# One core, two transformer blocks: the first stage in another order, and two modulation pieces summed by TensorE

## What is computed

```python
cond = jax.nn.silu(c)
mod = (cond @ w_ada[l] + b_ada[l])[:, None, :]
sh1, sc1, g1, sh2, sc2, g2 = jnp.split(mod, N_MOD, axis=-1)
h = x * (1.0 + sc1) + sh1
z = h @ w_in[l] + b_in[l]
z_u, z_v, z_h, z_g = jnp.split(z, split_pts, axis=-1)
```

## Time and profile before

| | |
|---|---|
| median of 3 executions | 2645.43 us (2644.23 to 2646.96) |
| profiled execution, its own time | 2642.59 us |
| its span, first to last instruction | 2641.3 us |
| TensorE busy, share of the span | 98% |
| VectorE / ScalarE busy | 70% / 49% |
| mean DMA rate over the span | 227 GB/s |
| mean granted TensorE clock | 0.995 |

### The profile page before, as it was taken

One profiled execution on the slowest core, in us unless ns is written; L12 is line 12 of the kernel. 1 busy time (PEld: TensorE's weight loads), 2 busy tenths in 40 slices (PEclk: granted clock), 3 DMA queues, 4 the chain that ended last, 5 costly groups with the idle time before them and its releaser, 6 DMA issues.

```text
span 2641.3 us, 31620 instructions
## 1 busy us (share of the span) xinstructions
PE 2599.3 (98%) x12546; PEld 2172.6 (82%) x12546; DVE 1846.0 (70%) x1927; ACT 1290.1 (49%) x1566; POOL 32.1 (1%) x55
## 2 busy tenths in 40 slices
PE   7899999999999999999999999999999999999999
PEld 3689988878888888888888888888888888988887
DVE  7879899988876644577776767755554665656565
ACT  2345544444444444555555544444444654555463
POOL 0000000000000000000000000000000000000000
PEclk9899999999999999999999999999999999999999
DMA  8998878798788755665656555555656556634554
GB/s 346 360 376 321 299 274 320 261 318 327 271 270 276 262 190 180 198 208 196 194 191 205 180 189 185 183 191 191 210 186 196 182 191 168 176 126 158 195 176 143
DMA packets 276584, 598.65 MB, mean 227 GB/s; under 512 B 21264, under 2 KB 46288, under 8 KB 260064
## 3 DMA queue, kind: packets, MB, share of 16 engines
q1 hardware_dynamic: 268272, 566.52, 63.1%
q0 software_dynamic: 4560, 21.56, 2.5%
q10 hardware_dynamic: 3616, 8.68, 0.9%
HBM read 586.24 MB, written 10.49 MB: 226 GB/s over the span
## 4 chain that ended last, share of the span: by engine, by line
PE 92%; DVE 5%; ACT 1%; DMA 1%; issue 1%; ACTq 0%; SPq 0%; DVEq 0%
PE ps L925 26%; PE ps L927 26%; PE ps L926 26%; PE ps L1050 2%; PE ps L1034 2%; PE ps L1036 2%; PE ps L1037 2%; DVE w_lo L2238 1%; DVE group_acc L2357 1%; DMA raw<-in_w_in 1%; PE ps L1433 1%; PE ps L1434 1%; PE ps L1435 1%; PE ps L1092 1%; PE ps L1085 0%
## 5 line engine op out<-in xcount | busy, mean ns | idle before, releaser
L2238 DVE TENSOR_TENSOR w_lo<-raw,w_hi 128x1024 fp32r<-128x1024 f32 x870 | 1050.3, 1221 | 673.2 <-ACT w_hi L1579 671.4
L1579 ACT CAST w_hi<-raw 128x1024 fp32r<-128x1024 f32 x870 | 906.6, 1051 | 1050.0 <-PE ps L927 913.3
L925 PE MATMUL ps<-w_lo,x_hi 128*128 128x512 f32 x2592 | 1021.2, 394 | 4.3 <-DVE w_lo L2238 2.8
L927 PE MATMUL ps<-w_hi,x_lo 128*128 128x512 f32 x2592 | 1011.6, 390 | 0.0
L926 PE MATMUL ps<-w_hi,x_hi 128*128 128x512 f32 x2592 | 1011.1, 390 | 0.0
L925 PEld LDWEIGHTS ps<-w_lo,x_hi 128*128 128x128 f32 x2592 | 488.3, 188 | 107.8 <-DVE w_lo L2238 4.6
L927 PEld LDWEIGHTS ps<-w_hi,x_lo 128*128 128x128 f32 x2592 | 488.1, 188 | 102.9
L926 PEld LDWEIGHTS ps<-w_hi,x_hi 128*128 128x128 f32 x2592 | 488.7, 189 | 100.3 <-issue 1.4
L2266 DVE SCALAR_TENSOR_TENSOR ada_acc<-raw,cond,ada_acc 128x2048 f32<-128x2048 f32 x64 | 150.1, 2345 | 2.0 <-DMA raw<-in_w_ada 1.0
L925 PE MATMUL ps<-w_lo,pooled_hi 128*128 128x512 f32 x384 | 150.2, 391 | 0.0
L927 PE MATMUL ps<-w_hi,pooled_lo 128*128 128x512 f32 x384 | 149.5, 389 | 0.0
(11 more groups left out here) (379 smaller groups left out, 2136.6 us busy)
## 6 DMA issues: line engine op xcount, KB each, us to landing
raw<-in_w_m SPq DMA_DIRECT2D x128, 1024.0 KB, 5.3
raw<-in_w_ada SPq DMA_DIRECT2D x64, 1024.0 KB, 5.7
raw<-in_pool_w_in SPq DMA_DIRECT2D x64, 1024.0 KB, 5.4
raw<-in_w_in SPq DMA_DIRECT2D x56, 1024.0 KB, 7.5
raw<-in_k_mod SPq DMA_DIRECT2D x32, 1024.0 KB, 6.6
raw<-in_pool_w_out SPq DMA_DIRECT2D x32, 1024.0 KB, 5.0
raw<-in_ple_w_gate SPq DMA_DIRECT2D x32, 1024.0 KB, 5.1
raw<-in_mla_w_in SPq DMA_DIRECT2D x24, 1024.0 KB, 5.1
```

Source lines behind the costliest of these rows:

```text
L925: mm(bank, xh, wl, start=start, stop=False)
L927: ins = mm(bank, xl, wh, start=False, stop=stop)
L1579: nc.scalar.copy(by_ktile(st, w_hi[st.half_slot(j, half)][:, 0:n]), raw_half(st, j, half)).then_inc(hi_split, 1)
L2238: tt(by_ktile(st, w_lo[slot][:, 0:n]), raw_half(st, j, half), by_ktile(st, w_hi[slot][:, 0:n].bitcast(F32)), ALU.subtract).then_inc(lo_spl ...
```

## The change

Three things change.

Pieces (1,2) and (2,6) are no longer added by VectorE. Their letter becomes `p`, and TensorE multiplies the landed data itself: `raw_block` is one single-column product of a 128x128 block with a column of `cond`, and 16 of them make a piece. The 16 of piece (1,2) stand between the products of unit (0,0), eight in each half, one after each of the first two products of a tile and k. Those of piece (2,6) stand in the second half of unit (1,1), two at each such place. They accumulate in the bank and columns of `group_sum`, whose products then add to them. The load four places behind a `p` waits for a new semaphore, `raw_summed`.

The banks of the filter products are spread (`spec_bank`), so that fewer of them wait for a copy. On TensorE the third filter's second part, the fourth filter and `group_sum(1)` change places: the sum comes first, and both parts of the fourth filter stand between the halves of units (0,2), (1,0) and (1,1). On VectorE `filter_part(3,0)` moves behind `group_sum(1)`, `filter_part(3,1)` behind the rest of unit (1,2), and the rest of unit (2,0) behind `group_scale(2)`. On ScalarE the rounding of unit (0,1) moves ahead of a spectrum copy.

Three of the four spectrum stores move from the end of the stage to where each spectrum is copied, the two first Gelus move into `in_h`, and on VectorE one modulation load and one output (`vu_third`) do so too.

```diff
@@ -121,7 +121,7 @@
 STREAM = [
-    ("first", 1, [("ggggggggw", ""), ("ggwggwggggw", ""), ("ggwggwggggw", ""), ("ggwggwgwgwgg", "wwww")]),
+    ("first", 1, [("ggggggggw", ""), ("ggwpgwggggw", ""), ("ggwggwggpgw", ""), ("ggwggwgwgwgg", "wwww")]),
     ("in_vu", 1, [("w", "aa")]), ("in_h", 2, A2), ("in_h2", 1, [("wwa", "wwaa")] * 2), ("in_g", 4, [("wwaa", "wwaa"), ("ww", "ww")]),
@@ -134,6 +134,9 @@
 FIRST_W = [(0, 0), (0, 1), (0, 2), (1, 0), (1, 1), (1, 2), (2, 0), (2, 1), (0, 3), (1, 3), (2, 2), (2, 3), (3, 0), (3, 1), (3, 2)]
+RAW_PIECE = (None, 2, 6, None)
@@ -415,6 +418,7 @@
     group_added = sem("group_added")
+    raw_summed = sem("raw_summed")
     ident_in = sem("ident_in")
@@ -547,16 +551,19 @@
     def group_ada(q, u):
-        return nth_load("g", 8 * q + u)
+        return [j for j, of in enumerate(ST["first"].pattern) if of != "w"][8 * q + u]
+    def added_by(q, u):
+        return sum(n != RAW_PIECE[p] for p in range(q + 1) for n in range(u if p == q else 8))
     def first_half(q, c, half):
...
     def spec_bank(it, m):
-        return 6 if it > 1 else 2 * m if it else 4 + 2 * m
+        return (2 * m, 4 + 2 * m, 2 + 2 * m, 6)[it]
     def sum_bank(q):
-        return 6 if q else 4
+        return 6 if q else 0
     WIDE = ("w_o", "m2", "pool_out", "w_out", "gate1")
@@ -599,8 +606,11 @@
                 used_g = st.freed("g", i, j)
+                used_p = st.freed("p", i, j)
                 if used_g > 0:
                     sync.wait_ge(group_added, used_g)
+                if used_p > 0:
+                    sync.wait_ge(raw_summed, used_p)
             if isinstance(src, tuple):
@@ -909,7 +919,7 @@
         mm = nc.tensor.matmul
-        def products(st, i, j, half, kt, hi, lo, banks, first, last, tiles=(0, 1)):
+        def products(st, i, j, half, kt, hi, lo, banks, first, last, tiles=(0, 1), between=None):
             slot = st.half_slot(j, half)
@@ -923,7 +933,11 @@
                     mm(bank, xh, wl, start=start, stop=False)
+                    if between:
+                        between(4 * c + 2 * t)
                     mm(bank, xh, wh, start=False, stop=False)
+                    if between:
+                        between(4 * c + 2 * t + 1)
                     ins = mm(bank, xl, wh, start=False, stop=stop)
@@ -1078,7 +1092,7 @@
             if it > 1:
-                pe.wait_ge(spec_copied, 2 * it + d)
+                pe.wait_ge(spec_copied, (2, 3, 4, 7)[2 * it + d - 4])
             for t in range(2):
@@ -1093,25 +1107,37 @@
             ins.then_inc(spec_mm, 1)
+        def raw_block(q, e, n):
+            st, u = ST["first"], RAW_PIECE[q]
+            j = group_ada(q, u)
+            col = e * 2 * CH + n * P
+            if e + n == 0:
+                pe.wait_ge(raw_full[st.slot(j)], st.landed(0, j))
+            ins = mm(ps[:, sum_bank(q), n:n + 1], raw[st.slot(j)][:, col:col + P], cond[:, 2 * u + e:2 * u + e + 1],
+                     start=e + n == 0, stop=False, skip_group_check=True)
+            if e == 1 and n == 7:
+                ins.then_inc(raw_summed, 1)
         def group_sum(q):
             if q == 0:
-                pe.wait_ge(spec_copied, 2)
-            elif q < 3:
-                pe.wait_ge(spec_copied, 6 + q)
-            else:
+                pe.wait_ge(spec_copied, 1)
+            elif q == 3:
                 pe.wait_ge(part_kept, 1)
-            pe.wait_ge(group_added, 8 * (q + 1))
+            whole = RAW_PIECE[q] is None
+            pe.wait_ge(group_added, added_by(q, 8))
             for n in range(8):
                 ins = mm(ps[:, sum_bank(q), n:n + 1], group_acc[q % 2][:, n * P:(n + 1) * P], ones[:, 0:1],
-                         start=True, stop=True)
+                         start=whole, stop=True, skip_group_check=not whole)
             ins.then_inc(group_summed, 1)
         st = ST["first"]
-        def group_half(q, c, half, first=None, last=None):
+        def group_half(q, c, half, first=None, last=None, between=None):
             pe.wait_ge(fm_lo if half else h_lo, q + 1)
             products(st, 0, group_weights(q, c), half, 4 * q + 2 * half, x_hi, x_lo, pair(c),
-                     q == 0 and half == 0 if first is None else first, q == 3 and half == 1 if last is None else last)
+                     q == 0 and half == 0 if first is None else first, q == 3 and half == 1 if last is None else last,
+                     between=between)
         def group_unit(q, c, first=None, last=None):
@@ -1136,21 +1162,28 @@
         pe.wait_ge(spec_copied, 4)
-        group_unit(0, 0)
+        for half in range(2):
+            group_half(0, 0, half, between=lambda n: raw_block(1, half, n))
         filter_product(2, 1)
+        pe.wait_ge(spec_copied, 5)
         group_half(0, 1, 0)
...
         group_half(0, 1, 1)
+        group_sum(1)
+        pe.wait_ge(spec_copied, 6)
+        group_half(0, 2, 0)
+        pe.wait_ge(mod_group, 2)
         filter_product(3, 0)
+        group_half(0, 2, 1)
         spectrum(3, 0)
-        group_sum(1)
-
-        group_unit(0, 2)
-        group_unit(1, 0)
+        group_half(1, 0, 0)
         filter_product(3, 1)
+        group_half(1, 0, 1)
+        spectrum(3, 1)
         group_half(1, 1, 0)
-        spectrum(3, 1)
-        group_half(1, 1, 1)
+        pe.wait_ge(spec_copied, 8)
+        group_half(1, 1, 1, between=lambda n: (raw_block(2, 0, n), raw_block(2, 1, n)))
         group_sum(2)
@@ -1693,18 +1726,21 @@
         group_hi(0, 1)
+        group_round(0, 1)
         spectrum_out(2, 0)
-        group_round(0, 1)
+        group_round(0, 2)
         spectrum_out(2, 1)
-        group_round(0, 2)
-        spectrum_out(3, 0)
+        spectrum_store(0)
         group_round(1, 0)
...
         group_round(1, 1)
+        spectrum_out(3, 0)
+        spectrum_store(1)
         group_round(1, 2)
         spectrum_out(3, 1)
+        spectrum_store(2)
         group_round(2, 0)
@@ -1739,11 +1775,8 @@
         def vu_end():
-            spectrum_store(0)
-            spectrum_store(1)
+            spectrum_store(3)
             columns_load()
-            gelu(0)
-            gelu(1)
         run_at(ST["in_vu"], 0, {2: vu_end})
@@ -1776,8 +1809,6 @@
                 gelu(3)
-                spectrum_store(2)
-                spectrum_store(3)
                 round_dft(0)
@@ -1787,8 +1818,8 @@
         st = ST["in_h"]
-        for i in range(2):
-            run(st, i, sgu_std)
+        run_at(st, 0, {2: lambda: (gelu(0), gelu(1)), 4: lambda: sgu_std(0, 0), 12: lambda: sgu_std(0, 1)})
+        run(st, 1, sgu_std)
         run(ST["in_h2"], 0, lambda i, c: conv_center(3 + c))
@@ -2344,7 +2375,7 @@
             if u:
-                dve.wait_ge(group_added, 8 * q + u)
+                dve.wait_ge(group_added, added_by(q, u))
             elif q >= 2:
@@ -2398,34 +2429,30 @@
         group_rest(0, 1)
-        add_first(1, 2)
+        add_first(1, 3)
         filter_part(2, 1)
-        add_first(1, 3)
-        add_first(1, 4)
         group_rest(0, 2)
-        add_first(1, 5)
-        filter_part(3, 0)
-        add_first(1, 6)
-        add_first(1, 7)
+        for u in range(4, 8):
+            add_first(1, u)
         group_rest(1, 0)
...
         group_lo(1, 1)
+        filter_part(3, 0)
         add_first(2, 1)
...
         add_first(2, 2)
+        group_rest(1, 2)
         filter_part(3, 1)
-        add_first(2, 3)
-        group_rest(1, 2)
-        for u in range(4, 8):
+        for u in (3, 4, 5, 7):
             add_first(2, u)
+        group_scale(2)
         group_rest(2, 0)
-
-        group_scale(2)
+        group_lo(2, 0)
         add_first(3, 0)
-        group_lo(2, 0)
         group_lo(2, 1)
@@ -2498,8 +2525,10 @@
         vu_out(1)
-        add_ada(st, 0, 2, 2, 1)
-        vu_out(2)
+        def vu_third():
+            vu_out(2)
+            add_ada(ST["in_vu"], 0, 2, 2, 1)
         def moments(src, width, t):
@@ -2523,7 +2552,7 @@
             tt(v, v, sgu_b[:], ALU.add).then_inc(vn_ready, 1)
-        run_at(ST["in_h"], 0, {4: lambda: vu_out(3), 6: lambda: split_dft(0), 8: sgu_norm, 12: lambda: conv_sides(0)}, lambda i, n: (2, 2 + n))
+        run_at(ST["in_h"], 0, {2: vu_third, 4: lambda: vu_out(3), 6: lambda: split_dft(0), 8: sgu_norm, 12: lambda: conv_sides(0)}, lambda i, n: (2, 2 + n))
         run_at(ST["in_h"], 1, {0: lambda: sgu_scaled(0), 4: lambda: conv_sides(1), 6: lambda: split_dft(2), 8: lambda: sgu_scaled(1),
...
```

## The result

| | before | changed |
|---|---|---|
| median of 13 executions | 2645.61 us (2642.37 to 2646.98) | 2651.13 us (2648.36 to 2653.78) |
| profiled execution, its own time | 2642.59 us | 2652.15 us |
| its span | 2641.3 us | 2650.8 us |

The ratio is 1.0022, with a 95% interval of 1.0015 to 1.0029: 5.5 us slower by the medians. The price of a step is therefore read from the profiles, the price of the whole from the medians.

A forecast was written before the change was run, and what follows sets the result against it. The prediction took TensorE, busy 98% of the span, as the bound. +3.6 us at `group_sum(2)` and +0.4 at the end of the stage made 2645.4 + 4.0 = 2649.5 us (rounded up by 0.1), range 2641 to 2656.

The forecast's parts named there:

- A block, 0.22 us: Each single-column product among wide ones costs TensorE 0.22 us, so a piece of 16 costs 3.5 us (bounds 1.8 and 7.0).
- the second rival: Blocks half hide, 1.8 us a piece: -1.7 us before `group_sum(1)` and again before `group_sum(2)`; total 2646, chance 0.2.
- `group_sum(1)` 2.0 us earlier: From 46 us on, VectorE stands 5.8 us before `filter_part(2,1)`, yet `group_sum(1)` starts at 73.4 instead of 75.4.
- TensorE's 32.1 us between the sums: From `group_sum(1)` to `group_sum(2)`, TensorE has 32.1 us of work, to 105.5, against VectorE's own 28.5 us.
- the loop of 3.6 us: Before `spectrum(3,1)`, TensorE stands 3.6 us for ScalarE's rounding, then VectorE's rest of unit (1,2) and `filter_part(3,1)`.
- The clock, +2.7: Low clock after TensorE's idle time before `group_sum(1)`: +1.7 us for that sum, +1.0 for five products behind (bounds 0, 4).
- The landing of (2,6), +2.0: At the blocks of piece (2,6), TensorE waits 2.0 us (bounds 1.3 and 3.9) for a load taking 5.5 us.
- `group_sum(2)` +3.6: `group_sum(2)` starts at 113.8 and ends at 115.6 against 112.0, shifting the kernel by +3.6 us.
- VectorE late by no more than a microsecond behind the sum: In the six units after `group_sum(2)`, VectorE is late for none by over a microsecond; TensorE stays the bound.
- The end of the stage, +0.4: The 1.60 us gap before `in_h` moves to its fifth half: +0.4 us (bounds -1.6 and +0.9).
- The first rival: The blocks before `group_sum(2)` run at 1.2 GHz: net +2 to +8 us on the forecast, 2652 to 2657; chance 0.2.
- The third: VectorE's relief comes through: `group_sum(1)` at 70, the second sum ending 4 us early; total 2639 to 2641, chance 0.13.

The follow-up runs named there:

- the new order alone: The changed kernel with pieces (1,2) and (2,6) added by VectorE again; ratio 0.9998 to the kernel before, median -1.7 us.
- piece (1,2) only: The changed kernel with only piece (1,2) on TensorE, (2,6) added by VectorE; ratio 1.0014 to the kernel before, median +2.9 us.
- the changed kernel kept busy: The changed kernel with 5 unused products on constants in TensorE's standing before `group_sum(1)`; 2649.23 us, ratio 1.0016 to the kernel before.
- piece (2,6) only: The changed kernel with only piece (2,6) on TensorE, (1,2) added by VectorE; ratio 1.0006 to the kernel before, median +1.6 us.
- filter first: The changed kernel with `filter_part(3,1)` ahead of the rest of unit (1,2) on VectorE; 2657.27 us, median of 5 executions.
- 17 unused products: The kernel before with 17 products on constants, into a bank nobody reads, ahead of `group_sum(2)` on TensorE; 2650.26 us.

## Why the prediction came out as it did

The total was right (2649.5 for 2651.1), and so were the direction and the mechanism, the work of VectorE given to an engine that becomes the bound between the sums. In the profile the terms differ more than the total does. That the total came so close is in part luck: two terms were off by 5.5 us too little and 2.0 us too much, and the profiled execution has a larger loss than the medians have.

- **A block, 0.22 us.** Right. In unit (0,0) the products of 49.73 to 57.7 stand as forecast: the filter product moved from 53.91 to 58.43, 3.6 us when the 0.92 us by which this profile starts later are taken off. In the half of 2.75 us with 16 blocks the window of 6.4 us gives 0.23 a block. That half of a block's price hides behind wide products (the second rival) isn't so.
- **`group_sum(1)` 2.0 us earlier.** 1.8. VectorE's standing of 5.8 us was 6.08.
- **TensorE's 32.1 us between the sums, and the loop of 3.6 us.** The standing is 3.53 us and where it was forecast. But the loop is not a cause by itself, as the new order alone shows: without the pieces there is room for it.
- **The clock, +2.7.** This is the term that was mis-sized. The sum took 1.7 us more, as taken. The half behind it ran low to its end, 5.3 us instead of 2.75, so 2.5 where I took 1.0. `spectrum(3,1)`, which I had only as a high bound, took 5.85 us (102.50 to the next half at 108.35); measured in the same way, start to start, a spectrum of the kernel before at full clock takes 3.03: 2.8. `group_sum(2)` itself took 3.08 instead of 1.84: 1.2. That is 8.2 us lost to the low level where I took 2.7. It is what this execution lost and not a fixed price: behind the same standing of 3.53 us the spectrum took 5.85 us here, 5.80 with piece (1,2) only, 5.72 with the changed kernel kept busy, 4.83 with the new order only and 3.13, so full clock, with piece (2,6) only. The run kept busy before `group_sum(1)` returned 4.3 us, of which 2.6 are of the sum and the half behind it. The spectrum of the kernel before and the product behind it:

```profile
58.40 3.59 PE L1092 MATMUL ps<-h_dif,dft 128*128 128x512 f32 x8
61.43 0.79 PE L925 MATMUL ps<-w_lo,x_hi 128*128 128x512 f32 x1
```

- **The landing of (2,6), +2.0.** Nothing, since the slow spectrum covered it: the load left at 105.02, 2.5 us into the spectrum as forecast, but TensorE came to the blocks 9.25 us after the spectrum's start and not 6.2. Where the spectrum runs at full clock, with piece (2,6) only, the term is right: the load leaves 2.5 us into it, lands 5.6 us later (I took 5.5), and TensorE waits 1.48 us. The 5.37 us of "filter first" are no measure of it, for there TensorE comes to the blocks 7.0 us earlier than in the changed kernel, counted from `group_sum(0)`, and the load leaves only 1.7 us earlier: it leaves at 101.90, TensorE is there at 103.37, and it lands 6.8 us after it left. Loads do take longer in the changed kernel. Their longest, between 38 and 120 us, is 9.1 to 10.5 us in the ten kernels with the new order, which have the stores moved, and 7.4 to 8.0 in the four with the old order. That the stores alone do it was not tried. Tile raw, 38 to 120 us, of the changed kernel, to be held against the earlier trace rows:

```profile
DMA to landing us min/median/max: 4.8/7.7/10.3
```

- **`group_sum(2)` +3.6.** +8.0 in this profile. The two errors, 5.5 too little for the clock and 2.0 too much for the landing, explain 3.5 of the 4.4 us. The medians moved by 5.5 and not by the 9.6 of this pair of profiles; how the low stretches fall differs between executions (the spectrum before `group_sum(1)` took 5.1 us instead of 3.7 in the profile with only the end of stage changed, where the code up to there is that of before, and 6.5 in the one with 17 unused products). Which part of the 8.0 us an average execution has stays open.
- **VectorE late by no more than a microsecond behind the sum.** 0.63 us before `group_sum(3)`.
- **The end of the stage, +0.4.** Between the starts of `group_sum(3)` and of the fifth half of `in_h` there are 43.8 us, against 44.6 before: -0.8, inside the bounds. The gap did move as forecast, and is 0.94 us. ScalarE, in the changed kernel, rounds the first halves of `in_h` straight behind 4.06 us of issuing; before, 5.74 us of issuing, the table load and two Gelus stood ahead of that the earlier trace rows:

```profile
182.19 2.00 ACT L1612 CAST w_hi<-raw 128x1024 fp32r<-128x1024 f32 x2 [4.06 <-issue]
...
198.00 3.89 ACT L1612 CAST w_hi<-raw 128x1024 fp32r<-128x1024 f32 x4
```

- **The first rival** (blocks at 1.2 GHz) did not come true in the changed kernel, where they ran at 1.00, but in both kernels that removed the standing ahead of the spectrum. "The half before is all wide", the argument against it, held as long as no standing lay between that half and the blocks, and once with 1.48 us of it; with 5.37 and with 1.34 us it failed. The argument for it, that narrow products don't hold the level, was drawn from one sum. Behind `group_sum(0)`, at 39.61 in the same profile, the clock stayed at 1.00. **The third** (the relief comes through) is what the new order without pieces has at `group_sum(1)`, 5.2 us earlier than before, and loses on the way to `group_sum(2)`.
- **What the reading left out.** The forecast names three stretches of idle time of the first stage. There is a fourth, 3.64 us before the spectrum at 70.08, where TensorE stands for VectorE's `filter_part`; the new order moves this filter, and the standing before `spectrum(3,1)` is of the same kind. The sum counts from `group_sum(1)` and isn't changed by it.

## What to carry to other kernels

Before work is moved off the engine that others wait for, add up what the receiving engine has to do between the same two points: 28.5 us against 32.1 said that the bound would change sides, and each piece then cost 3.2 to 3.5 us, what its blocks take. Ask too what the relieved engine will wait for next: with one piece on TensorE its saved passes went into a wait for a landing. Idle time in front of a wait is not free time for work that stands further ahead in the queue: the blocks stood ahead of a filter product that VectorE was waiting for, and not in the gap. And a gap of TensorE that is cured upstream may reopen in front of narrow products, where it can cost more: in one profile the standing of 5.37 us and then 5.5 us of low clock. Before a term is called right or wrong from one profile, look at how much two profiles of the same code differ there, here by up to 2.3 us.

## What the runs showed of the hardware

A single-column product of 128x128 float32 between wide products costs 0.23 us at 2.4 GHz (6.4 us for a half with 16 of them, 2.75 without) and about 0.44 at 1.2 GHz (the half of 11.7 us). Nothing of this was seen to hide behind the wide product next to it. The Trainium skill ("TensorE: Matmul & The Clock Gate", "LDWEIGHTS (loading the stationary operand)") gives the time of a load in nanoseconds as its columns divided by 1.2, so by estimate 107 ns for 128 columns and 0.21 us for two. The trace has two records a product and agrees in the price, 0.23 us; its load records last 0.19 us each and overlap, so a load by itself is not shown. A full float32 product of 512 columns costs 0.86 us, two records of 0.43 (34 records in 14.75 us).

The clock behind a standing or behind narrow products differed from profile to profile. Sixteen narrow products between twelve wide ones ran at 1.00 over their 6.4 us in the changed kernel. With a standing ahead of them they ran at 0.50 behind 5.37 us, fell to it a good microsecond after 1.34 us, and stayed at 1.00 behind 1.48 us. Sixteen in a row, with no standing ahead, fell to 1.2 GHz after 2.9 us.
